# A scan of sixteen chunks with its samples, its ends in a new order, and the last stage's loads and lows moved

## What is computed

```python
def wkv7_step(state, inp):
    r_t, w_t, k_t, v_t, a_t, b_t = inp
    sa = jnp.einsum('bhij,bhj->bhi', state, a_t)
    state = (state * w_t[:, :, None, :] + sa[..., None] * b_t[:, :, None, :]
             + v_t[..., None] * k_t[:, :, None, :])
    y = jnp.einsum('bhij,bhj->bhi', state, r_t)
    return state, y
...
    y = ((y - mu) * lax.rsqrt(var + LNX_EPS) * lnx_g.astype(f32).reshape(H, N)
         + lnx_b.astype(f32).reshape(H, N))
    out = ((y + bonus).reshape(B, S, D).astype(h.dtype) * g) @ w_o
...
def sq_relu_mlp(h, w_up, w_down):
    return jnp.square(jax.nn.relu(h @ w_up)) @ w_down
...
        xp = xp + mp[2] * op
        hp = pre_norm(xp, norm2_g[i], mp[3], mp[4])
        xp = xp + mp[5] * sq_relu_mlp(hp, mlp_up[i], mlp_down[i])
```

## Time and profile before

| | us |
|---|---|
| median of 3 runs | 2743.39 |
| lowest, highest | 2740.34, 2746.11 |
| the profiled execution | 2751.72 |
| its span | 2749.7 |
| PE busy | 2586.4 (94%) |
| DVE, ACT, POOL busy | 1458.8 (53%), 1123.9 (41%), 895.8 (33%) |
| mean granted clock of TensorE | 0.973 |

### The profile page before, as it was taken

One profiled execution on the slowest core, in us unless ns is written; L12 is line 12 of the kernel. 1 busy time (PEld: TensorE's weight loads), 2 busy tenths in 40 slices (PEclk: granted clock), 3 DMA queues, 4 the chain that ended last, 5 costly groups with the idle time before them and its releaser, 6 DMA issues. The chain is left out here.

```text
span 2749.7 us, 52825 instructions
## 1 busy us (share of the span) xinstructions
PE 2586.4 (94%) x21466; PEld 2433.3 (88%) x21466; DVE 1458.8 (53%) x2782; ACT 1123.9 (41%) x2250; POOL 895.8 (33%) x725
## 2 busy tenths in 40 slices
PE   4989999989889999999999999998988999999998
PEld 2769898878789999999999998887988999999997
DVE  6358777246677211212212354875686666565665
ACT  5447633325455312202202343665465443434334
POOL 1122212147721221122211302112168874445442
PEclk7999999999989999999999999998999999999998
DMA  8878768788781322222222312212222321111112
GB/s 335 327 261 259 233 238 250 218 192 199 193 262 47 106 79 70 92 92 76 88 91 77 105 57 64 72 46 78 66 62 85 93 89 51 47 51 51 51 47 78
DMA packets 383096, 342.29 MB, mean 124 GB/s; under 512 B 115526, under 2 KB 352522, under 8 KB 375916
## 3 DMA queue, kind: packets, MB, share of 16 engines
q1 hardware_dynamic: 351788, 298.20, 35.5%
q10 hardware_dynamic: 25408, 21.41, 2.7%
q0 software_dynamic: 5664, 19.33, 1.9%
HBM read 258.75 MB, written 78.78 MB: 123 GB/s over the span
## 5 line engine op out<-in xcount | busy, mean ns | idle before, releaser
L1405 PE MATMUL t_acc<-t_area,wH 128*128 128x258 f32 (+1 forms) x1552 | 465.4, 300 | 16.0 <-DVE shared L1823 5.3
L1406 PE MATMUL t_acc<-t_area,wH 128*128 128x258 f32 (+1 forms) x1552 | 460.1, 296 | 0.0
L1407 PE MATMUL t_acc<-t_area,wL 128*128 128x258 f32 (+1 forms) x1552 | 459.9, 296 | 0.0
L556 POOL TENSOR_TENSOR wL<-raw,wH 128x1024 fp32r<-128x1024 f32 x61 | 146.2, 2398 | 666.9 <-ACT wH L681 666.9
L1405 PEld LDWEIGHTS t_acc<-t_area,wH 128*128 128x128 f32 x1552 | 295.7, 191 | 22.7 <-issue 12.1
L1406 PEld LDWEIGHTS t_acc<-t_area,wH 128*128 128x128 f32 x1552 | 295.7, 191 | 0.2
L1407 PEld LDWEIGHTS t_acc<-t_area,wL 128*128 128x128 f32 x1552 | 295.3, 190 | 0.1
L1698 DVE SCALAR_TENSOR_TENSOR X<-t_acc,mod,X 128x258 f32<-128x258 f32 (+4 forms) x456 | 237.5, 532 | 105.6 <-PE t_acc L1407 74.8
L1360 POOL TENSOR_TENSOR wL<-raw,wH 128x512 fp32r<-128x512 f32 x126 | 168.4, 1343 | 258.1 <-ACT wH L1536 257.0
L577 PE MATMUL t_acc<-twoH,wH 128*128 128x344 f32 x744 | 239.8, 322 | 2.6 <-DVE twoL L902 1.6
L579 PE MATMUL t_acc<-twoH,wL 128*128 128x344 f32 x744 | 237.5, 319 | 0.0
(11 more groups left out here) (561 smaller groups left out, 6684.7 us busy)
## 6 DMA issues: line engine op xcount, KB each, us to landing
ada_ring<-in_ada_w SPq DMA_DIRECT2D x24, 1024.0 KB, 9.3
shared<-in_ada_w SPq DMA_DIRECT2D x24, 1024.0 KB, 6.3
raw<-in_mlp_up SPq DMA_DIRECT2D x84, 256.0 KB, 2.9
t_plain<-in_mlp_down SPq DMA_DIRECT2D x84, 256.0 KB
raw<-in_mlp_down SPq DMA_DIRECT2D x32, 512.0 KB, 4.2
raw<-in_mlp_up SPq DMA_DIRECT2D x30, 512.0 KB, 4.1
kvrb_hx<-hx_saved ACTq DMA_DIRECT2D x16, 516.5 KB, 4.7
kvr_work<-scr_L SPq DMA_DIRECT2D x16, 516.0 KB, 5.8
```

What stands on the lines that cost most here:

```text
L556: pool.tensor_tensor(low, raw_of(w), high.bitcast(F32), ALU.subtract).then_inc(s_low, 1)
L1405: pe.matmul(out, high, h, start=begin, stop=False, skip_group_check=True)
L1406: pe.matmul(out, high, l, start=False, stop=False, skip_group_check=True)
L1407: return pe.matmul(out, low, h, start=False, stop=end, skip_group_check=True)
```

## The change

At the scan's start the samples' vectors are stored by ACT and loaded by SP, behind the BK loads of chunks 2 and 3. In every chunk DVE does `products` and `outputs` behind the updates of S, and POOL does `centred` ahead of the samples' work; `removed` is cut in three (`removed`, `read`, `faded`). At the scan's end the parts of the last chunk's sample step are put between the turns' scaling, with `faded` behind all of it, and DVE's norm of the samples is cut in two. The affine step, adds and rounding of the tail stage's first two row blocks, and both parts of w_o's panels 0 and 1, are made in the scan, the affine step before the last chunk's Y copy, the panels' parts in the drain. The tail stage begins with panels 0 and 1 by blocks 0 and 1, first what needs no low part of the blocks. In the last stage X is loaded by half quarters, the combined pieces are made in another order, POOL starts round 1 when all 28 lows are made, and from round 1 on it makes P2's low ahead of the two sums. Tensors are placed anew to make room for this. The core of the diff:

```diff
+                for k in range(2):
+                    for m in range(2):
+                        high, low = place("o", m)
+                        pe.wait_ge(s_ph, k + 1)
+                        pe.wait_ge(s_lowD, m + 1)
+                        pe.matmul(acc[m][:, 0:TT], high[:, k, :], HH[:, k, third[0]], start=(k == 0), stop=False)
+                        pe.matmul(acc[m][:, 0:TT], low[:, k, :], HH[:, k, third[0]], start=False, stop=False)
+                    for m in range(2):
+                        pe.wait_ge(s_pl, k + 1)
+                        pe.matmul(acc[m][:, 0:TT], place("o", m)[0][:, k, :], HL[:, k, third[0]], start=False, stop=False)
+                for k, m in [(0, 2), (1, 2), (2, 0), (2, 1), (2, 2)] + [(k, 3) for k in range(3)] + [(k, m) for k in range(3, DB) for m in range(4)]:
...
-            affine(0)
-            high(0)
-            affine(1)
-            prepared(0)
-            high(1)
             high(2)
...
-            adds(0)
+                dve.sem_inc(s_ph, 2)
+                dve.sem_inc(s_lowD, 2)
+                dve.sem_inc(s_high, 2)
+                dve.sem_inc(s_paff, 2)
+                dve.sem_inc(s_padd, 4)
+            prep_low(0)
+            prep_low(1)
             dve.wait_ge(net.s_lateY, 32)
-            own_low(0)
-            prep_low(0)
-            adds(1)
-            own_low(1)
-            prep_low(1)
...
-    LOWS_FIRST = {"P1": (14, 20), "P2": (20, 24), "P6": (24, 28)}
+    HIGHS_FIRST = {"P1": (14, 16), "P2": (20, 24), "P6": (24, 28)}
+    HIGHS_THEN = {"P1": (16, 20)}
+    LOWS_FIRST = {"P1": (14, 16), "P2": (16, 24), "P5": (24, 28)}
...
             def load_x(q):
-                sp.wait_ge(s_pl, (q + 1) * DB)
-                sp.dma_start(X[:, :, quarter[q]], net.x_saved[:, :, quarter[q]]).then_inc(s_x[q], 16)
+                for h in range(2):
+                    b = slice(4 * h, 4 * h + 4)
+                    sp.wait_ge(s_pl, q * DB + 4 * h + 4)
+                    sp.dma_start(X[:, b, quarter[q]], net.x_saved[:, b, quarter[q]]).then_inc(s_x[q][h], 16)
...
+                if r == 1:
+                    pool.wait_ge(s_cl, 28)
                 low(weight_at["p", r, "P1"])
+                if r:
+                    low(weight_at["p", r, "P2"])
...
-                low(weight_at["p", r, "P2"])
+                if r == 0:
+                    low(weight_at["p", r, "P2"])
...
-                if m == 0:
-                    dve.wait_ge(s_x[q], 16)
+                if m % 4 == 0:
+                    dve.wait_ge(s_x[q][m // 4], 16)
...
+        act.wait_ge(self.s_tev, 2)
+        act.dma_start(self.net.sSmp.rearrange("i s c -> (i s) c"), self.rows[:]).then_inc(self.s_rows, 16)
+
+    def vectors(self, sp):
+        sp.wait_ge(self.s_rows, 16)
         for i in range(5):
-            pool.dma_start(self.vec[:, i, :], self.net.sSmp[i].rearrange("s (h d) -> (s h) d", d=HD)).then_inc(self.s_vec, 16)
+            sp.dma_start(self.vec[:, i, :], self.net.sSmp[i].rearrange("s (h d) -> (s h) d", d=HD)).then_inc(self.s_vec, 16)
...
+                elif s == 1:
+                    smp.vectors(sp)
...
+            sp.wait_ge(s_next, 64)
+            sp.wait_ge(s_piece, 96)
             smp.store(sp)
...
             def work(c, k, i, last):
                 scaled(c, k)
+                centred(c, k)
                 pool.wait_ge(smp.s_S, i * 16 + 16)
-                pool.wait_ge(smp.s_value, 16)
-                pool.wait_ge(smp.s_vec, 80)
+                pool.wait_ge(smp.s_vec, 96)
                 smp.values(pool, c)
-                centred(c, k)
-                smp.removed(pool, c)
+                if not last:
+                    smp.removed(pool, c)
+                    smp.read(pool, c)
+                    smp.faded(pool, c)
...
-            smp.vectors(pool)
             for c in range(NCH):
                 work(c, c % BODY, c // BODY, c == NCH - 1)
-            for k in range(Y_LAG):
+            scaled(NCH, 0)
+            smp.removed(pool, NCH - 1)
+            centred(NCH, 0)
+            smp.read(pool, NCH - 1)
+            for k in range(1, Y_LAG):
                 scaled(NCH + k, k)
-                if k == 0:
-                    centred(NCH, 0)
+            smp.faded(pool, NCH - 1)
...
+                if left == 1:
+                    for q in range(2):
+                        affine(q)
+                if left == 0:
+                    for q in range(2):
+                        rounded(q)
...
-                smp.outputs(dve, c)
                 mean(c, k, c)
-                smp.products(dve, c)
+                if not left:
+                    for q in range(2):
+                        adds(q)
                 dve.wait_ge(s_D, c + 1)
                 dve.tensor_tensor(pD[:], pD[:], S[:], ALU.add).then_inc(s_sum, 1)
-                if not last:
+                if left:
                     masked(c + 1, 1 - g, 1)
                 dve.wait_ge(s_sum, c + 1)
                 for half in range(2):
                     b = slice(4 * half, 4 * half + 4)
                     dve.tensor_tensor(S[:, b], pD[:, b], net.pend[:, b, bass.ds(c, 1)].to_broadcast([128, 4, HD]), ALU.mult).then_inc(s_S, 1)
+                if left:
+                    smp.products(dve, c)
+                    smp.outputs(dve, c)
...
+            inverse(NCH)
+            smp.products(dve, NCH - 1)
+            mean(NCH, 0, NCH)
+            dve.wait_ge(s_yi, NCH + 1)
+            variance(NCH)
+            smp.outputs(dve, NCH - 1)
+            own_low(0)
+            inverse(NCH + 1)
+            dve.wait_ge(s_yi, NCH + 2)
+            variance(NCH + 1)
+            smp.outputs(dve, NCH)
+            smp.centre(dve)
+            inverse(NCH + 2)
+            smp.spread_of(dve)
+            smp.scaled(dve)
+            own_low(1)
```

131 lines of the change are left out of this document (82 added, 49 removed).

## The result

The changed kernel took 2758.49 us (median of 10 runs, 2750.05 to 2770.5) against 2750.01 of the kernel before (10 runs beside them), a ratio of 1.0035 with a 95% interval of 1.002 to 1.005. It is slower by some 9 us; the forecast was 4 us faster. Taken a second time beside other runs of the kernel before it was 1.0038 (1.0024 to 1.0053).

The account below looks back on a forecast made before the run. TensorE, busy nearly all of the span, was taken as the bound. Scan start -7.0, scan end and tail +4.0, rounds 0 to 1 -6.9, half rounds +6.7, first rounds 0.8 gained: -4.0 off 2743.4, so 2739.4 us; range 2731.5 to 2747.5.

Parts of the forecast that it names:

- A: Scan start: DVE masks at once and the clock stays up, until POOL is late next; -7.0 us (-9 to -4).
- B + C: Scan end and tail stage together: a later store, partly won back by the tail's start; +4.0 us (+1.5 to +6.5).
- D1: Last stage, round 0 to 1: X in halves and reordered lows bring TensorE's hidden product sooner; -6.9 us (-8.2 to -4).
- D2: Half rounds 5 to 9: the sums behind P2's low delay d0, 1.35 us a round; +6.7 us (0 to +8).
- first rounds, P2's sooner low: First rounds of the last stage: part of P2's sooner low should stay as a gain of 0.8 us.
- Rival 1: Half rounds: P2's panel lands sooner, so the sums don't hold up TensorE; total -9.5 us, 2734; chance 0.17.
- v = 595: Scan start: late end for the vectors' landing, behind all SP has issued; the gain is then only 4.3 us.
- rival 3: Slower: late vectors, late store, a smaller round-1 gain and costlier half rounds together; total +6.5 us, 2750; chance 0.12.
- B: Scan end: the samples' store is issued later, behind faded, and the next stage waits for its landing; +5.1 us (4 to 6.5).
- C: Tail stage: work moved into the drain lets TensorE start with the stage; 1.1 us of the 5.1 come back.

Follow-up runs that it names:

- e7: The changed kernel, but from round 1 on POOL makes P2's low between the two sums, not ahead of them: 2744.58 us, ratio 0.9978 to the kernel before.
- e13: The kernel before with only DVE's products and outputs of the samples moved behind the scaling of S in every chunk: 2742.75 us, ratio 0.9975.
- e14: The kernel before with the edits of e13 and d1 together and nothing else: 2739.43 us, ratio 0.9958.
- e5: The changed kernel with P2's low behind the sums again and the samples' state stored in two parts: 2736.09 us, ratio 0.9945 to the kernel before.
- d1: The kernel before with X by half quarters, the new order of highs and lows, and POOL's wait for 28 lows: 2740.84 us, ratio 0.9965.
- e12: The kernel before with X loaded by half quarters and nothing else changed: 2745.95 us, ratio 0.9989.
- e2: The kernel before with only POOL's order changed, P2's low ahead of the two sums from round 1 on: 2764.57 us, ratio 1.0053.

## Why the prediction was wrong

**Base.** The forecast 2739.4 was taken off a median of three runs, 2743.39; ten runs gave 2750.01. That alone is 6.6 us, more than the forecast change. The rest of this section compares changes: -4.0 forecast, +8.5 measured.

**Sum.** The terms, in their own places (a mean over the traces that have the part, less a mean over those that haven't):

| term | forecast | ends | measured in the traces |
|---|---|---|---|
| A, scan start | -7.0 | -9 to -4 | -8.1 (161.1 to 153.0) |
| B + C, scan end and tail | +4.0 | +1.5 to +6.5 | +6.0 (189.6 to 195.6) |
| D1, rounds 0 and 1 | -6.9 | -8.2 to -4 | -6.3 over rounds 0 to 9 (229.4 to 223.1) |
| D2, half rounds | +6.7 | 0 to +8 | +19.2 (223.1 to 242.3) |
| first rounds, P2's sooner low | -0.8 | none given | within D2: only round 1's P2 comes sooner, and its d0 doesn't |
| total | -4.0 | -11.9 to +4.1, the stated range | +10.8 by these terms, +8.5 by the medians |

Rival 1's total of -9.5 doesn't follow from its own terms either: without D2 they give -10.7.

**The step that failed is D2.** The place, the direction and the mechanism were as written: POOL stands still until P2's high is there, the sums follow, and TensorE waits for d0's low. The size, +6.7, was a third of the measured +19.2, for three reasons.

1. The count. The prediction priced five rounds and took three, which it calls 2 to 4, at zero, since "there P2 comes sooner and d0 later". By POOL's sums the three are rounds 3 to 5, and the kernel has nine half rounds, 1 to 9, in which the pair of lows is made. P2 doesn't come sooner in those three. The stop ahead of P2 stands against POOL's low, but POOL's low waits for ACT's high, and that for its panel; the sums had fitted into this wait. In the changed kernel the stops before P2 are still there (2.84 us in round 4, where it was 3.39), and 2.4 us before d0 come on top in each of nine rounds. The bracket names the last releaser; whether POOL was late by its own work or by its input stands in the row of POOL, and that row, with its own bracket, I had read for one later round only.
2. The size in a round. 1.35 was 5.16 us of POOL's four operations of 1.29, less TensorE's start and a gap. The sums took 1.50 and 1.27 and d0's low 1.45, and DVE's operations beside them 1.39 in place of 0.43 (the half round above). From the end of ACT's high to d0 it was 5.52 us, where the prediction had 5.16 and the kernel before 3.51, and the 0.26 that it let be absorbed was not: the stop rose by 2.41 - 0.28 = 2.1.
3. The rounds behind. From round 5 to 9 a half round became 1.7 to 2.9 us longer, 2.3 in the mean, a bit more than its stop. That POOL's later lows release the next loads later would explain the difference; it is argued, not shown.

What the range should have held is this estimate: nine rounds by the bound of two sums, 9 x 2.5 = 22 us, with the 2.5 of e7's rule. The upper end of 8 came from five rounds. The count of places was taken as certain while only the price had ends.

**A was right.** DVE's mask no longer waits, the clock holds, and POOL's scaling of chunk 1 is next late, by 1.48 us. The vectors' landing in SP's queue was the doubt; `values` began 15.0 us behind the first U product, where they had 14.3, so the end v = 595 and the part of rival 3 that hung on it fall. Against the rule of the Trainium skill ("DMA: Bandwidth & Descriptors", "Queues, rings and completion order"), which made A -4.3 if the loads lost a turn of their own: the loads from SP's queue landed 3.0 us after their last issue in the changed kernel, and from POOL's 5.2 before (read from the start of `values`, which waits for them). Over all traces it is 1.4 to 3.0 us in SP's queue and 4.1 to 5.8 in POOL's. No loss by the move is seen. e13 shows what the prediction didn't say: most of the gain comes from DVE's two lines, and all the rest of the new order at the scan's start, the move of the loads with it, is worth at most some 1.5 us (154.5 for the scan's first half in e13 and e14, 153.0 with the rest).

**B was right in its mechanism and size:** the store's issue 8.2 us later against the last D product (7 forecast), the wait 6.1 for the landing (7.2), the stage +6.0 later (5.1). e5 shows the gate. **C** gave less back than I took: TensorE starts 2.2 us later than before against the same mark, and at its stop on POOL at 780.04 (786.41 before) it is 7.5 us late, not 4. The loads there move with the stage's start in full: the DMA share is 0.97 to 1.06 for 30 us behind it, and was 0.93 to 1.06 before. TensorE waits 5.17 us for the third block's low part, which DVE can only make when its loads have landed. I had argued just that and still taken 1.1 us back. The drain grew too, by 1.6 us: its last turn begins 13.8 us behind the last D product, where it was 12.2. Its second turn waits 5.59 us for POOL, with removed, centred and read of the samples now between two scalings; the prediction put faded behind the scalings but forgot that others came between.

DVE's adds in the scan's last chunk took 0.51 to 1.24 us each beside POOL. The exclusive lock of the Trainium skill ("SBUF — State Buffer", "SBUF: two separate sides") fits these and the 1.39 of the half rounds. In the drain it fell on POOL: beside DVE's own_low of 1.22 us the first operation of `removed` took 1.59, where it had 0.61 before, and that lies between the two scalings that TensorE's 5.59 us stand for:

```profile
733.59 1.59 POOL L3349 TENSOR_TENSOR step_t<-step_sa,step_vec 128x256 f32<-128x256 f32 x1
```

In the half rounds it can be in the 0.4 us by which the first sum and d0's low were over 1.29.

**D1 was right.** Round 1's hidden product came 6.9 us sooner in d1 and 6.3 in the changed kernel, for 6.9 forecast, and in the changed kernel TensorE waited there for POOL's low of d0, as written. That the figure was met so closely is in part luck, since 2020.8 was only the middle between two bounds. e12 splits the 9.1 us won ahead of that: X in halves 3.7 and, by difference, the order of lows with POOL's wait 5.4.

**Chances.** The slower side had 0.10, in rival 3 with four parts that had to come together. D2 came at more than twice its bound of 8, with B + C near theirs (+6.0 of 6.5), and the gains of A and D1 came in full beside them.

## What to carry to other kernels

A wait in the row of an engine that is not the bottleneck may be the cover of the work queued before it: move such work behind the wait and it stands on the path. Count the places where a new order will stop the bottleneck by the structure (once for every round in which the pair of operations is issued), and only then price one. And a row that says "waits for POOL" has to be followed one engine further, since whether POOL was busy or itself waiting decides what moving its work does.

## What the runs showed of the hardware

The traces of the same code differ by more than most parts of this change. The unchanged stretch ahead of the scan took between 482.4 and 494.1 us in sixteen traces, and the turn from attention to the last stage 13.1 us in three and 8.0 to 8.4 in the others. The latter is TensorE's granted clock. Just ahead of the last stage's first product, which begins at 1902.0 in both, the kernel before and e2 with the same code there show (columns as in the earlier trace rows):

```profile
1895.00:1900.00 5.00, 5.00 (x31) 4.61 (x31) 1.30 (x6) 0.97 (x1) 0.00 (x0) 0.50 0.00 0
```

```profile
1895.00:1900.00 5.00, 5.00 (x59) 4.63 (x59) 0.80 (x4) 1.41 (x2) 0.00 (x0) 1.00 0.00 0
```

In these 5 us it is the lower level, 1.2 GHz, in the one and the full clock in the other, 31 matmuls against 59, and no edit lies between them. So a single trace of each kernel, taken by its total, would have called this change 1.7 us faster. Compare traces by stretches between the same instructions, and totals by the medians of many runs.
